# First stage of a fused block: rows scaled before a plain transpose, two blocks' columns formed by TensorE, filler products, another order of transfers

## The chip, the cores and the metric

The kernel runs on one core of a Trainium2 chip. The time is that of one execution on the device in microseconds. Five engines run their own instruction streams and meet at semaphores: TensorE (matrix products; its weight loads are listed apart), VectorE, ScalarE, GpSimd (POOL in the views), and SyncE (SP), which here only issues transfers.

## What is computed

One layer of a network on 1024 tokens of width 1024, float32. The first stage, the only one that the change touches, is the normalised input with a modulation computed from the condition `c`, times the first projections:

```python
mod = silu(c) @ ada_w + ada_b
sh1, sc1, g1, sh2, sc2, g2 = split(mod, 6)
h = rms_norm(x) * (1.0 + sc1) + sh1
y = mlstm_mixer(h, ml_w_in, ml_b_if, ml_norm_w, ml_w_out)
x = x + g1 * y
h = rms_norm(x) * (1.0 + sc2) + sh2
x = x + g2 * swiglu(h, ffn_w_gate_up, ffn_w_down)
out = rms_norm(x) * final_norm_w
```

`mlstm_mixer` projects `h` to queries, keys, values, an output gate and eight gate columns for four heads, runs a chunked recurrence and projects back.

## The kernel before, in words

The program is written out by hand: every engine has its own list of instructions, and the order in each list is the order of the code. Waits are explicit (`wait_ge` on a semaphore). Nothing is planned at run time. Transfers of the first stage are issued by SP in the order of its code and share the same DMA engines; a few small ones go out from ScalarE's and POOL's own queues.

The first stage works on eight rows of x (128 tokens by 1024 columns each, tile `xin`) and on eight blocks `k` of 128 columns of the transposed input (`xnT`, 128 columns by 1024 tokens, in two halves of 512 tokens).

- **Rows.** For row t ScalarE squares it and adds up (`square`, L916), copies a transposed bank of row t-2 out of PSUM (`evac_xT`, L926), and takes the root (`root`, L920). VectorE takes the reciprocal (`inverse`, L1402) and multiplies the identity by it (`diagonal`, L1418, tile `diag`, two buffers). TensorE then multiplies the row by the diagonal, eight products of 128 by 128 into two banks (L2136): it scales and transposes at once. VectorE copies the other bank out (`evac_xT`, L1423). A bank pair is used again two rows later.
- **Columns.** Block k needs a scale and a shift for each of its 128 columns of h: `silu(c) @ ada_w` for two sets of 128 columns. The weights of block k are one tile `ada0` of 1 MB (128 by 8 by 256, four buffers). VectorE multiplies its eight slices by the entries of `cact` and adds them (`sum1`, L1387, L1394, L1398, nine operations into `acc0`), and TensorE adds up over the partitions by two products with a column of ones (`mod_columns`, L2122). ScalarE adds the bias (`mod_columns`, L934). The sums of blocks 0 and 1 are spread between VectorE's rows, those of blocks 2 to 7 follow the rows.
- **Modulation.** ScalarE applies the columns to each half of block k (`modulate`, L944) and rounds it to the short float32 form that TensorE takes in one pass (`hH`, L948); POOL subtracts to get the rest (`hL`, L729). Every later product is made of three: high by high, low by high, high by low.
- **First products.** For each block TensorE does for both halves two times three products (queries and keys of head 0, L2088) and two for the gate columns (L2162), 16 in all, and ahead of block k it forms the columns of block k+1. It begins when the rows are all transposed, the half block is there (`m_L`), POOL has the first half weight unit's parts (`w_L`, L716, L722) and the gates' weights (`wg_L`, L735, L737).

SP's order (L468 to L483): rows 0, 1, 2 of x; the tile of block 0; rows 3 to 6; the tile of block 1; the gates' weights; row 7; the first half of weight unit 0; the tiles of blocks 2 and 3; the second half of unit 0; and then the tiles 4 to 7, each when its buffer is free (L464). `c` itself is loaded from ScalarE's queue (L908). A tile's buffer is free when VectorE's sum over it is done.

The wait that orders a row's part on TensorE is on the diagonal; on its banks, on both copies of two rows before:

```python
for t in range(NT):
    pe.wait_ge(n_hn, t + 1)
    for j in range(2):
        if t >= 2:
            pe.wait_ge(xT_ok[j], t - 1)
```

Of the kernel before, what the change touches and what calls it, by code (L numbers as in the profile page):

```python
# [21 lines left out]
ALU = mybir.AluOpType  # L22
ACT = mybir.ActivationFunctionType

P = 128
D = 1024
S = 1024
NT = S // P
KD = D // P
# [16 lines left out]
N1 = KD + 1  # L46
GATE_ROWS = 36
N_FOLDED = 7

# [79 lines left out]
def build(nc, x, c_col, ada_first, ada_first_b, ada_rest, ada_rest_b, w_units, w_gates, b_if, norm_w, final_w, out,  # L129
          scan_rows, mod_rows):  # L130
    with ExitStack() as ctx:
# [49 lines left out]
        th = at("th", [P, 2, DV], Z0 + 6144)  # L181
        diag = at("diag", [P, 2, P], Z0 + 6144)
        gate = at("gate", [P, 2, DV], Z0 + 8192)
# [270 lines left out]
        def _(sp):  # L454
# [7 lines left out]
            def ada_first_tile(k):  # L462

                if k >= 4:  # L464
                    sp.wait_ge(acc0_ok, N1 * (k - 3))
                sp.dma_start(ada0[:, k % 4], ada_first[k]).then_inc(ada0_in[k % 4], 16)

            for t in range(NT):  # L468
                sp.dma_start(xin[:, t, :], x[t]).then_inc(x_in[t], 16)
                if t == 2:  # L470
                    ada_first_tile(0)
                if t == 6:
                    ada_first_tile(1)
                    sp.dma_start(wg_raw[:], w_gates).then_inc(wg_in, 16)
            load_unit(0, (0,))
            for k in range(2, KD):
                ada_first_tile(k)
                if k == 3:
                    load_unit(0, (1,))
                if k == 6:  # L480
                    load_unit(1, (0,))
# [215 lines left out]
        def _(pool):  # L697
# [28 lines left out]
            def low1(k, half):  # L726
# [3 lines left out]
                                        ALU.subtract).then_inc(m_L, 1)  # L730

            pool.wait_ge(wg_in, 16)
            pool.wait_ge(wg_zero, 1)
# [3 lines left out]
            nc.gpsimd.tensor_tensor(wgL, wg_raw[:], wgH.bitcast(F32), ALU.subtract).then_inc(wg_L, 1)  # L737
            first_high()
            for c in range(4):
                first_low(c)  # L740
            for k in range(KD):
                for half in range(2):
                    low1(k, half)
                    if 3 <= 2 * k + half <= 6:
                        first_low(1 + 2 * k + half)
            pool.wait_ge(acc0_ok, N1 * KD)

# [148 lines left out]
        def _(act):  # L896
# [10 lines left out]

            act.dma_start(craw[:], c_col).then_inc(c_in, 16)  # L908
            act.dma_start(b1[:], ada_first_b).then_inc(b1_in, 16)
# [40 lines left out]
            for t in range(NT):  # L950
                act.wait_ge(x_in[t], 16)
                if t:
                    act.wait_ge(n_ms, t)
                square(t, xin[:, t, :])
                if t >= 2:
                    evac_xT(t - 2)
                root(t)
            act.wait_ge(b1_ok, 1)
            mod_columns(0)
            modulate(0, 0)  # L960
            evac_xT(NT - 2)
            evac_xT(NT - 1)
            modulate(0, 1)
# [399 lines left out]
        def _(dve):  # L1363
# [12 lines left out]
            def sum1(k, first=0, last=KD):  # L1376

                base = k * N1
                even, odd = (SUM_BANK[:, i * 2 * P:(i + 1) * 2 * P] for i in range(2))
                if first == 0:  # L1380
                    dve.wait_ge(ada0_in[k % 4], 16 * (k // 4 + 1))
                    if base:
                        dve.wait_ge(acc0_ok, base)
                for r in range(first, last):
                    acc1 = (even, odd)[r % 2]
                    if r < 2:
                        nc.vector.tensor_scalar(acc1, ada0[:, k % 4, r, :], cact[:, r:r + 1], None,  # L1387
                                                ALU.mult).then_inc(acc0_ok, 1)
                    else:
                        dve.wait_ge(acc0_ok, base + r - 1)  # L1390
                        if r == KD - 1 and k >= 2:
                            dve.wait_ge(mod1_mm, k - 1)
                        dst = acc0[:, k % 2, :] if r == KD - 1 else acc1
                        nc.vector.scalar_tensor_tensor(dst, ada0[:, k % 4, r, :], cact[:, r:r + 1], acc1,  # L1394
                                                       ALU.mult, ALU.add).then_inc(acc0_ok, 1)
                if last == KD:
                    dve.wait_ge(acc0_ok, base + KD)
                    nc.vector.tensor_tensor(acc0[:, k % 2, :], acc0[:, k % 2, :], even, ALU.add).then_inc(acc0_ok, 1)  # L1398
# [15 lines left out]

            def diagonal(t):
                if t >= 2:
                    dve.wait_ge(n_tr, 2 * (t - 1))
                nc.vector.tensor_scalar(diag[:, t % 2, :], ident[:], rstd[:, t:t + 1], None, ALU.mult).then_inc(n_hn, 1)  # L1418

            def evac_xT(t):  # L1420

                dve.wait_ge(n_tr, 2 * t + 2)
                nc.vector.tensor_copy(four_of(xnT, 1, t),  # L1423
                                      XT_BANKS[2 * (t % 2) + 1][:].rearrange("p (k n) -> p k n",
                                                                             n=P)).then_inc(xT_ok[1], 1)

# [5 lines left out]
            for t in range(NT):  # L1432
                inverse(t)
                diagonal(t)
                if t >= 2:
                    evac_xT(t - 2)
                if 1 <= t <= 3:
                    sum1(0, 3 * (t - 1), min(3 * t, KD))
                if t >= 5:
                    sum1(1, 2 * (t - 5), 2 * (t - 4))  # L1440
            sum1(1, 6)
            evac_xT(NT - 2)
            evac_xT(NT - 1)
            for k in range(2, KD):
                sum1(k)
# [638 lines left out]
        def _(pe):  # L2084
# [31 lines left out]
            def mod_columns(k):  # L2116

                pe.wait_ge(acc0_ok, N1 * (k + 1))
                if k:
# [6 lines left out]
            def start():  # L2126

                pe.wait_ge(set_ok, 3)
                pe.wait_ge(const_ok, 5)
                for t in range(NT):  # L2130
                    pe.wait_ge(n_hn, t + 1)
                    for j in range(2):
                        if t >= 2:
                            pe.wait_ge(xT_ok[j], t - 1)
                        for k in range(4):
                            ins = nc.tensor.matmul(XT_BANKS[2 * (t % 2) + j][:, k * P:(k + 1) * P],  # L2136
                                                   xin[:, t, (4 * j + k) * P:(4 * j + k + 1) * P], diag[:, t % 2, :],
                                                   start=True, stop=True)
                        ins.then_inc(n_tr, 1)
                    if t == 4:  # L2140
                        mod_columns(0)
                mod_columns(1)
                pe.wait_ge(wg_L, 1)
                ws = unit_weights(0, 2 * DK)
                for k in range(KD):
# [4 lines left out]
                    for half in range(2):  # L2150
# [5 lines left out]
                        for m in range(2):  # L2156
                            ins = three(QK_BANKS[2 * half + m][:], tuple(w[:, k, m * DK:(m + 1) * DK] for w in ws),
                                        hs, k, k, last)
                            if last:
                                ins.then_inc(qk_mm, 1)  # L2160
                        for i in range(2):
                            ins = nc.tensor.matmul(OP[half][:], gate_weights[:, k, :], hs[i], start=(k == 0 and i == 0),  # L2162
# [387 lines left out]
```

## Time and profile before

| | |
|---|---|
| median of 3 runs | 1089.62 us (1089.36 to 1090.15) |
| the profiled execution, its own time | 1089.08 us |
| its span, first to last instruction | 1087.30 us |
| TensorE busy | 1072.2 us (99%) |
| VectorE, ScalarE, POOL busy | 728.5, 447.4, 167.8 us |
| mean DMA rate over the span | 165 GB/s |

Busy time of an engine over the whole span says little here, since the stages differ. The chain of waits follows the work that ended last back to the start; the timelines give each engine's instructions in order with the idle time ahead of them and what ended it; the windows view gives busy time and transfer rate of a stretch. A row "x16" is sixteen instructions taken together, and its duration reaches from the first start to the last end.

### The profile page before, as it was taken

The page shows a single profiled execution, that of the slowest core. Times are in us where ns is not written, and L with a number is a line of the kernel's source. Part 1 is how long each engine was busy: PE and PEld are TensorE (multiplying, and loading weights), DVE is VectorE, ACT ScalarE, POOL GpSimd, SP SyncE. Part 2 cuts the span into 40 slices and gives each one's busy share as a digit, 9 for nine tenths or more (in the row PEclk, how much of TensorE's full clock was granted, in tenths as well). Part 3 has the DMA queues.
Part 4 walks back from the last instruction along what each step waited for, and adds up shares of the span by engine and source line. Part 5 has one row for each costly group of instructions (what it writes and reads, how often), then busy time and mean ns, then how long its engine had stood idle before and what let it go on. Part 6 is the DMA issues. An engine that isn't in the chain of part 4 may idle for free.

```text
span 1087.3 us, 14704 instructions
## 1 busy us (share of the span) xinstructions
PE 1072.2 (99%) x5139; PEld 901.3 (83%) x5139; DVE 728.5 (67%) x1289; ACT 447.4 (41%) x824; POOL 167.8 (15%) x149
## 2 busy tenths in 40 slices
PE   6999999999999999999999999999999999999997
PEld 6888888888888888888888888888888888888886
DVE  6846777477478627888666676756667465844666
ACT  7852232322234216754343333334333325444435
POOL 3752221212326423310000000000000000000000
PEclk9999999999999999999999999999999999999999
DMA  9425453532543423115536435453643879665544
GB/s 377 171 78 170 127 189 97 150 126 59 169 126 91 165 75 136 59 43 200 187 114 214 154 124 177 154 177 116 211 158 113 304 269 396 216 193 193 194 155 156
DMA packets 88091, 178.94 MB, mean 165 GB/s; under 512 B 8377, under 2 KB 31545, under 8 KB 86993
## 3 DMA queue, kind: packets, MB, share of 16 engines
q1 hardware_dynamic: 87104, 176.63, 48.3%
q0 software_dynamic: 480, 1.09, 0.3%
q8 instruction: 41, 0.67, 0.3%
q10 hardware_dynamic: 432, 0.27, 0.1%
q14 instruction: 34, 0.27, 0.1%
HBM read 135.97 MB, written 40.16 MB: 162 GB/s over the span
## 4 chain that ended last, share of the span: by engine, by line
PE 98%; DVE 1%; DMA 0%; ACT 0%; issue 0%; DVEq 0%
PE OP L2388 27%; PE OP L2088 21%; PE O L2388 15%; PE ST L2388 6%; PE DC L2388 5%; PE AD L2388 5%; PE O L2088 3%; PE ST L2088 3%; PE AD L2088 2%; PE DC L2088 2%; PE O L2245 1%; PE O L2261 1%; PE DC L2261 1%; PE ST L2136 1%; PE ST L2228 1%; PE OP L2162 1%
## 5 line engine op out<-in xcount | busy, mean ns | idle before, releaser
L1853 DVE TENSOR_TENSOR dL<-dF,dH 128x1024 fp32r<-128x1024 f32 x77 | 93.0, 1223 | 69.8 <-ACT dH L1235 69.1
L2088 PE MATMUL OP<-wH,hH 128*128 128x512 f32 (+1 forms) x360 | 135.0, 375 | 0.1
L2088 PE MATMUL OP<-wH,hL 128*128 128x512 f32 (+1 forms) x360 | 132.0, 367 | 0.0
L2088 PE MATMUL OP<-wL,hH 128*128 128x512 f32 (+1 forms) x360 | 131.7, 366 | 0.0
L1235 ACT CAST dH<-dF 128x1024 fp32r<-128x1024 f32 x77 | 79.8, 1051 | 89.1 <-DMA dF<-w_units 37.8
L2388 PE MATMUL OP<-tH,wsH 128*128 128x512 f32 x264 | 102.7, 389 | 0.0
L2388 PE MATMUL OP<-tL,wsH 128*128 128x512 f32 x264 | 102.7, 389 | 0.0
L2388 PE MATMUL OP<-tH,wsL 128*128 128x512 f32 x264 | 102.7, 389 | 0.0
L2088 PEld LDWEIGHTS OP<-wH,hL 128*128 128x128 f32 x360 | 67.8, 188 | 11.3
L2088 PEld LDWEIGHTS OP<-wH,hH 128*128 128x128 f32 x360 | 67.9, 189 | 10.3 <-issue 0.3
L2088 PEld LDWEIGHTS OP<-wL,hH 128*128 128x128 f32 x360 | 68.0, 189 | 10.0
L1147 ACT CAST wsH<-wsF 128x512 fp32r<-128x512 f32 x88 | 53.1, 620 | 47.3 <-DVE wsF L1769 39.9
L1147 ACT CAST wsH<-raw 128x512 fp32r<-128x512 f32 x66 | 38.8, 620 | 74.8 <-DMA raw<-w_units 58.6
L2388 PE MATMUL O<-hH,wsH 128*128 128x512 f32 x176 | 68.5, 389 | 0.0
L2388 PE MATMUL O<-hL,wsH 128*128 128x512 f32 x176 | 68.5, 389 | 0.0
L2388 PE MATMUL O<-hH,wsL 128*128 128x512 f32 x176 | 68.5, 389 | 0.0
L1808 DVE TENSOR_TENSOR wsL<-wsF,wsH 128x512 fp32r<-128x512 f32 x88 | 58.2, 686 | 14.4 <-ACT wsH L1147 14.4
L1764 DVE TENSOR_TENSOR wsF<-raw 128x512 f32<-128x512 f32 x21 | 14.5, 692 | 74.2 <-DMA raw<-w_units 64.8
L824 POOL TENSOR_TENSOR hg<-hc,gate 128x256 f32<-128x256 f32 x32 | 36.5, 1142 | 164.8 <-DVE gate L1597 164.8
L768 POOL DMA_DIRECT2D g2b<-mod_rows x1 | 0.6, 602 | 375.8 <-DVE wsL L1808 375.8
L2388 PEld LDWEIGHTS OP<-tH,wsL 128*128 128x128 f32 x264 | 49.6, 188 | 10.4
L2388 PEld LDWEIGHTS OP<-tL,wsH 128*128 128x128 f32 x264 | 49.5, 188 | 10.3
(344 smaller groups left out, 2642.2 us busy)
## 6 DMA issues: line engine op xcount, KB each, us to landing
raw<-w_units SPq DMA_DIRECT2D x76, 512.0 KB, 4.8
dF<-act_mid SPq DMA_DIRECT2D x77, 256.0 KB, 2.9
ada<-ada_rest SPq DMA_DIRECT2D x64, 256.0 KB, 2.9
wst<-w_units SPq DMA_DIRECT2D x44, 256.0 KB, 4.9
down_mid<-wst SPq DMA_DIRECT2D x22, 512.0 KB, 3.2
dF<-down_mid SPq DMA_DIRECT2D x44, 256.0 KB, 2.9
dF<-w_units SPq DMA_DIRECT2D x33, 256.0 KB, 5.6
ada<-ada_first SPq DMA_DIRECT2D x8, 1024.0 KB, 10.1
```

The source lines that it names most:

```text
L824: nc.gpsimd.tensor_tensor(hg[:, c - 1, h * DV:(h + 1) * DV], hc[:, (c - 1) % 2, :], gate[:, (c - 1) % 2, :], ALU.mult).then_inc(hg_ok, 1)
L1147: nc.scalar.copy(wsH[n % 2][W_SLOT.index(q)][:], src).then_inc(c_H, 1)
L1235: nc.scalar.copy(dH[g][:], dF[g][:]).then_inc(d_H, 1)
L1764: nc.vector.tensor_tensor(f[5][:], gate_up_block(0, 1), gate_up_block(1, 1), ALU.add).then_inc(c_sum, 1)
L1808: nc.vector.tensor_tensor(wsL[n % 2][i][:], src, wsH[n % 2][i][:].bitcast(F32), ALU.subtract).then_inc(c_L, 1)
L1853: nc.vector.tensor_tensor(dL[g][:], dF[g][:], dH[g][:].bitcast(F32), ALU.subtract).then_inc(d_L, 1)
L2088: ins = nc.tensor.matmul(out_ap, lhs[a], rhs[b], start=(n == 0 and i == 0), stop=(last and i == 2))
L2136: ins = nc.tensor.matmul(XT_BANKS[2 * (t % 2) + j][:, k * P:(k + 1) * P], xin[:, t, (4 * j + k) * P:(4 * j + k + 1) * P], diag[:, t % 2, : ...
L2162: ins = nc.tensor.matmul(OP[half][:], gate_weights[:, k, :], hs[i], start=(k == 0 and i == 0), stop=(last and i == 1))
L2228: nc.tensor.matmul(ST[c % 2][:, 0:P], kT[:, toks], qT[:, toks], start=True, stop=True)
L2261: ins = nc.tensor.matmul(out_ap, lhs[a], rhs[b], start=(first and i == 0), stop=(i == 2))
L2388: ins = nc.tensor.matmul(out_ap, lhs[a], rhs[b], start=(first and i == 0), stop=(last and i == 2), skip_group_check=True)
```

## The change

Six edits, all in the first stage:

1. `c` is loaded first on SP's queue and no longer from ScalarE's. SP then loads rows 0 to 5, the tile of block 0, rows 6 and 7, the first half of unit 0, the gates' weights, the tiles of blocks 1 and 2, the second half of unit 0, and the tiles of blocks 3 to 7.
2. VectorE multiplies the whole row by the reciprocal in place (`scale_row`), and TensorE transposes it plainly; the tile `diag` is gone.
3. The columns of blocks 0 and 1 come from TensorE alone (`columns_from_weights`): for each of a block's two sets eight products, the weight tile's slices as stationary operand and one column of `cact` as the moving one. The sets of block 0 stand behind rows 4 and 5, both of block 1 behind row 7. VectorE's sums begin with block 2, and the semaphore counts are shifted by two blocks.
4. TensorE multiplies a tile of ones by itself, 14 times ahead of row 0 and twice behind rows 0 to 3 and row 6 (`keep_warm`); nothing reads the results.
5. ScalarE's copies of a bank stand behind the root and stop at row 4; VectorE copies both banks of rows 5 to 7. VectorE's copies belong to row t-1 instead of t-2.
6. POOL splits the half unit before the gates' weights, and TensorE waits for the gates' weights only ahead of the first gate product.

```diff
+BY_PE = 2
+X_BY_ACT = 5
+WARM = 14
+FILL = 2
...
             def ada_first_tile(k):
-                if k >= 4:
-                    sp.wait_ge(acc0_ok, N1 * (k - 3))
+                if k >= 4 + BY_PE:
+                    sp.wait_ge(acc0_ok, N1 * (k - 3 - BY_PE))
+                elif k >= 4:
+                    sp.wait_ge(mod1_mm, k - 3)
                 sp.dma_start(ada0[:, k % 4], ada_first[k]).then_inc(ada0_in[k % 4], 16)
+            sp.dma_start(craw[:], c_col).then_inc(c_in, 16)
             for t in range(NT):
                 sp.dma_start(xin[:, t, :], x[t]).then_inc(x_in[t], 16)
-                if t == 2:
+                if t == 5:
                     ada_first_tile(0)
-                if t == 6:
-                    ada_first_tile(1)
-                    sp.dma_start(wg_raw[:], w_gates).then_inc(wg_in, 16)
             load_unit(0, (0,))
-            for k in range(2, KD):
+            sp.dma_start(wg_raw[:], w_gates).then_inc(wg_in, 16)
+            for k in range(1, KD):
                 ada_first_tile(k)
-                if k == 3:
+                if k == 2:
                     load_unit(0, (1,))
...
+            first_high()
+            for c in range(4):
+                first_low(c)
             pool.wait_ge(wg_in, 16)
...
-            first_high()
-            for c in range(4):
-                first_low(c)
...
-            act.dma_start(craw[:], c_col).then_inc(c_in, 16)
...
                 square(t, xin[:, t, :])
-                if t >= 2:
+                root(t)
+                if 2 <= t <= X_BY_ACT + 1:
                     evac_xT(t - 2)
-                root(t)
             act.wait_ge(b1_ok, 1)
             mod_columns(0)
             modulate(0, 0)
-            evac_xT(NT - 2)
-            evac_xT(NT - 1)
             modulate(0, 1)
...
-            def diagonal(t):
-                if t >= 2:
-                    dve.wait_ge(n_tr, 2 * (t - 1))
-                nc.vector.tensor_scalar(diag[:, t % 2, :], ident[:], rstd[:, t:t + 1], None, ALU.mult).then_inc(n_hn, 1)
+            def scale_row(t):
+                nc.vector.tensor_scalar(xin[:, t, :], xin[:, t, :], rstd[:, t:t + 1], None, ALU.mult).then_inc(n_hn, 1)
...
             for t in range(NT):
                 inverse(t)
-                diagonal(t)
-                if t >= 2:
-                    evac_xT(t - 2)
-                if 1 <= t <= 3:
-                    sum1(0, 3 * (t - 1), min(3 * t, KD))
-                if t >= 5:
-                    sum1(1, 2 * (t - 5), 2 * (t - 4))
-            sum1(1, 6)
-            evac_xT(NT - 2)
-            evac_xT(NT - 1)
-            for k in range(2, KD):
+                scale_row(t)
+                if t:
+                    if t - 1 >= X_BY_ACT:
+                        evac_xT(t - 1, 0)
+                    evac_xT(t - 1, 1)
+            evac_xT(NT - 1, 0)
+            evac_xT(NT - 1, 1)
+            for k in range(BY_PE, KD):
                 sum1(k)
...
+                def columns_from_weights(k, m):
+                    pe.wait_ge(ada0_in[k], 16)
+                    pe.wait_ge(c_act, 1)
+                    if k:
+                        pe.wait_ge(mod1_ok, 2 * k)
+                    for r in range(KD):
+                        ins = nc.tensor.matmul(DC[:, 2 * k + m:2 * k + m + 1], ada0[:, k, r, m * P:(m + 1) * P],
+                                               cact[:, r:r + 1], start=(r == 0), stop=(r == KD - 1))
+                    if m == 1:
+                        ins.then_inc(mod1_mm, 1)
+                def keep_warm(n):
+                    for _ in range(n):
+                        nc.tensor.matmul(OP[0][:, 0:P], ones[:], ones[:], start=True, stop=True)
+                keep_warm(WARM)
                 for t in range(NT):
                     pe.wait_ge(n_hn, t + 1)
...
-                            ins = nc.tensor.matmul(XT_BANKS[2 * (t % 2) + j][:, k * P:(k + 1) * P],
-                                                   xin[:, t, (4 * j + k) * P:(4 * j + k + 1) * P], diag[:, t % 2, :],
-                                                   start=True, stop=True)
+                            ins = nc.tensor.transpose(XT_BANKS[2 * (t % 2) + j][:, k * P:(k + 1) * P],
+                                                      xin[:, t, (4 * j + k) * P:(4 * j + k + 1) * P], ident[:])
                         ins.then_inc(n_tr, 1)
-                    if t == 4:
-                        mod_columns(0)
-                mod_columns(1)
-                pe.wait_ge(wg_L, 1)
+                    if t in (4, 5):
+                        columns_from_weights(0, t - 4)
+                    elif t < NT - 1:
+                        keep_warm(FILL)
+                for m in range(2):
+                    columns_from_weights(1, m)
```

What the edits do to the order on the engines shows at three places. First TensorE from row 4 to the first product. `ST` and `O` are the banks of the transposed rows, `DC` the bank of the columns, `OP` that of the fillers. Before:

```order
L2136 MATMUL ST<-diag,xin 128x128 x8
L2122 MATMUL DC<-ones,acc_75 128x1 x2
L2136 MATMUL O<-diag,xin 128x128 x8
L2136 MATMUL ST<-diag,xin 128x128 x8
L2136 MATMUL O<-diag,xin 128x128 x8
L2122 MATMUL DC<-ones,acc_75 128x1 x2
L2088 MATMUL O<-hH,wH 128x512
```

Now:

```order
L2152 MATMUL ST<-ident,xin 128x128 x8
L2135 MATMUL DC<-cact,ada_55 128x1 x8
L2152 MATMUL O<-ident,xin 128x128 x8
L2135 MATMUL DC<-cact,ada_55 128x1 x8
L2152 MATMUL ST<-ident,xin 128x128 x8
L2143 MATMUL OP<-ones 128x128 x2
L2152 MATMUL O<-ident,xin 128x128 x8
L2135 MATMUL DC<-cact,ada_55 128x1 x16
L2086 MATMUL O<-hH,wH 128x512
```

The two products per block with ones became sixteen per block with the weights, and they stand between the rows and ahead of the first product. Second SP's transfers up to the tiles that wait (`xin` rows of x, `ada_55` the tiles of the blocks, `raw` half weight units). Before:

```order
L469 DMA xin<-x 128x1024 x3
L466 DMA ada_55<-ada_first 128x2048
L469 DMA xin<-x 128x1024 x4
L466 DMA ada_55<-ada_first 128x2048
L474 DMA wg_raw<-w_gates 128x288
L469 DMA xin<-x 128x1024
L460 DMA raw<-w_units 128x1024
L466 DMA ada_55<-ada_first 128x2048 x2
L460 DMA raw<-w_units 128x1024
```

Now:

```order
L473 DMA craw<-c_col 128x8
L475 DMA xin<-x 128x1024 x6
L471 DMA ada_55<-ada_first 128x2048
L475 DMA xin<-x 128x1024 x2
L463 DMA raw<-w_units 128x1024
L479 DMA wg_raw<-w_gates 128x288
L471 DMA ada_55<-ada_first 128x2048 x2
L463 DMA raw<-w_units 128x1024
```

The tile of block 0 moved behind rows 3 to 5, that of block 1 behind row 7, half a unit and the gates. Third VectorE at the end of the rows and the first whole sum. Before:

```order
L1402 RECIPROCAL rstd<-sd 128x1
L1418 TENSOR_SCALAR diag<-ident,rstd 128x128
L1423 COPY xnT<-O 128x4x128
L1394 SCALAR_TENSOR_TENSOR AD<-ada_55,cact,AD 128x256 x3
L1394 SCALAR_TENSOR_TENSOR acc_75<-ada_55,cact,AD 128x256
L1398 TENSOR_TENSOR acc_75<-acc_75,AD 128x256
L1423 COPY xnT<-ST 128x4x128
L1423 COPY xnT<-O 128x4x128
L1387 TENSOR_SCALAR AD<-ada_55,cact 128x256 x2
```

Now:

```order
L1403 RECIPROCAL rstd<-sd 128x1
L1417 TENSOR_SCALAR xin<-xin,rstd 128x1024
L1424 COPY xnT<-ST 128x4x128 x2
L1424 COPY xnT<-O 128x4x128 x2
L1388 TENSOR_SCALAR AD<-ada_55,cact 128x256 x2
```

The sums between the rows are gone, and two more copies stand behind the last row.

## Rows read from the trace of the kernel before

**Rows 1.** Chain of waits that ended last, page, whole program, share by engine.

```profile
PE 98%; DVE 1%; DMA 0%; ACT 0%; issue 0%; DVEq 0%
```

**Rows 2.** TensorE's timeline: start, duration (us), line, operation, count.

```profile
8.62 3.75 PE L2136 MATMUL ST<-diag,xin 128*128 128x128 f32 x16 [8.62 <-DVE diag L1418]
...
21.78 1.95 PE L2136 MATMUL ST<-diag,xin 128*128 128x128 f32 x16
23.57 1.95 PE L2136 MATMUL O<-diag,xin 128*128 128x128 f32 x16
...
26.07 0.48 PE L2088 MATMUL O<-hH,wH 128*128 128x512 f32 x1
...
30.84 0.48 PE L2088 MATMUL O<-hH,wH 128*128 128x512 f32 x1
...
34.58 0.50 PE L2122 MATMUL DC<-ones,acc 128*128 128x1 f32 x4
34.94 0.49 PE L2088 MATMUL O<-hH,wH 128*128 128x512 f32 x1
```

**Rows 3.** Weight loads' timeline, same columns; in brackets the idle time before.

```profile
28.18 0.19 PEld L2088 LDWEIGHTS ST<-hH,wH 128*128 128x128 f32 x1 [0.47 <-POOL hL L729]
...
30.37 0.52 PEld L2122 LDWEIGHTS DC<-ones,acc 128*128 128x128 f32 x4 [0.49 <-DVE acc L1398]
```

**Rows 4.** ScalarE's timeline, first rows of x.

```profile
4.77 0.21 ACT L911 ACTIVATE cact<-craw 128x8 f32<-128x8 f32 x1 [1.80 <-DMA craw<-c_col]
...
6.40 1.04 ACT L916 ACTIVATE junk<-xin 128x1024 f32<-128x1024 f32 x1
...
7.56 0.29 ACT L920 ACTIVATE sd<-ms,eps 128x1 f32<-128x1 f32 x1
7.76 1.04 ACT L916 ACTIVATE junk<-xin 128x1024 f32<-128x1024 f32 x1
...
10.71 0.59 ACT L926 COPY xnT<-ST 128x512 f32<-128x512 f32 x1 [0.44 <-PE ST L2136]
11.19 0.30 ACT L920 ACTIVATE sd<-ms,eps 128x1 f32<-128x1 f32 x1
```

**Rows 5.** DMA issues near 0.8 and 6.8 us: KB, us to landing.

```profile
xin<-x SPq DMA_DIRECT2D x1, 512.0 KB, 3.8
craw<-c_col ACTq DMA_DIRECT2D x1, 4.0 KB, 4.0
...
ada<-ada_first SPq DMA_DIRECT2D x1, 1024.0 KB, 17.6
```

**Rows 6.** Windows view, 12.2 to 26: length, engines' busy time, PEclk, DMA, GB/s.

```profile
12.20:26.00 13.80, 13.71 (x121) 13.52 (x120) 12.80 (x33) 11.81 (x27) 6.29 (x8) 1.00 1.03 418
```

**Rows 7.** SP's timeline of DMA issues.

```profile
0.75 1.35 SPq L469 DMA_DIRECT2D xin<-x  x3
...
6.75 1.43 SPq L466 DMA_DIRECT2D ada<-ada_first  x2
```

**Rows 8.** VectorE's timeline: a diagonal, first operations of sums 2 and 3.

```profile
8.19 0.29 DVE L1418 TENSOR_SCALAR diag<-ident,rstd 128x128 f32<-128x128 f32 x1
...
26.66 0.86 DVE L1387 TENSOR_SCALAR AD<-ada,cact 128x256 f32<-128x256 f32 x2
...
30.43 0.87 DVE L1387 TENSOR_SCALAR AD<-ada,cact 128x256 f32<-128x256 f32 x2
```

**Rows 9.** Line view of the later scaling of rows: min, median, max ns.

```profile
L1945 DVE TENSOR_SCALAR xs<-x,rstd x8: 753/754/1033, 409.2 to 452.8; 128x1024 f32<-128x1024 f32 x8
```

**Rows 10.** TensorE's timeline, later plain transposes, four each.

```profile
418.05 0.60 PE L2112 MATMUL O<-ident,xs 128*128 128x128 f32 x4
418.49 0.60 PE L2112 MATMUL ST<-ident,xs 128*128 128x128 f32 x4
```

**Rows 11.** POOL's timeline: half unit's cast, first low half of block 0.

```profile
20.32 1.04 POOL L716 CAST wH<-raw 128x1024 fp32r<-128x1024 f32 x1 [1.24 <-DMA raw<-w_units]
...
24.19 1.27 POOL L729 TENSOR_TENSOR hL<-xnT,hH 128x512 fp32r<-128x512 f32 x1
```

More of the change, by code:

```diff
@@ L181, in build @@
         th = at("th", [P, 2, DV], Z0 + 6144)
-        diag = at("diag", [P, 2, P], Z0 + 6144)
         gate = at("gate", [P, 2, DV], Z0 + 8192)
@@ L745, in _ @@
                         first_low(1 + 2 * k + half)
-            pool.wait_ge(acc0_ok, N1 * KD)
+            pool.wait_ge(acc0_ok, N1 * (KD - BY_PE))
             nc.gpsimd.memset(rows[0:GATE_ROWS, A_, :], 0.0).then_inc(rows_set, 1)
@@ L1376, in sum1 @@
             def sum1(k, first=0, last=KD):
-                base = k * N1
+                base = (k - BY_PE) * N1
                 even, odd = (SUM_BANK[:, i * 2 * P:(i + 1) * 2 * P] for i in range(2))
@@ L1390, in sum1 @@
                         dve.wait_ge(acc0_ok, base + r - 1)
-                        if r == KD - 1 and k >= 2:
+                        if r == KD - 1 and k >= 2 + BY_PE:
                             dve.wait_ge(mod1_mm, k - 1)
@@ L1413, in low, with evac_xT @@
                                             ALU.subtract).then_inc(n_L, 1)
-            def diagonal(t):
-                if t >= 2:
-                    dve.wait_ge(n_tr, 2 * (t - 1))
-                nc.vector.tensor_scalar(diag[:, t % 2, :], ident[:], rstd[:, t:t + 1], None, ALU.mult).then_inc(n_hn, 1)
[L1420 to L1425, printed above, removed]
+            def scale_row(t):
+                nc.vector.tensor_scalar(xin[:, t, :], xin[:, t, :], rstd[:, t:t + 1], None, ALU.mult).then_inc(n_hn, 1)
+            def evac_xT(t, j):
+                dve.wait_ge(n_tr, 2 * t + j + 1)
+                if j == 0 and t == X_BY_ACT:
+                    dve.wait_ge(xT_ok[0], t)
+                nc.vector.tensor_copy(four_of(xnT, j, t),
+                                      XT_BANKS[2 * (t % 2) + j][:].rearrange("p (k n) -> p k n",
+                                                                             n=P)).then_inc(xT_ok[j], 1)
             dve.wait_ge(b1_in, 16)
@@ L2116, in mod_columns @@
             def mod_columns(k):
-                pe.wait_ge(acc0_ok, N1 * (k + 1))
+                pe.wait_ge(acc0_ok, N1 * (k + 1 - BY_PE))
                 if k:
@@ L2160, in start @@
                                 ins.then_inc(qk_mm, 1)
+                        if k == 0 and half == 0:
+                            pe.wait_ge(wg_L, 1)
                         for i in range(2):
```

## The prediction

> **What bounds the kernel now.** The chain of waits comes first: 98% of it is TensorE [rows 1], so a microsecond counts only where TensorE's own sequence starts sooner or loses a gap. TensorE's timeline of the start [rows 2] shows where that can be. It stands until 8.62 us, transposes eight rows until 25.5, starts the first product at 26.07, and from 30.84 repeats a period of 4.10 us (30.84 to 34.94), block after block. Two gaps lie between [rows 3]: 0.47 us for POOL's low half of block 0, and 0.49 us for VectorE's sum of block 2, whose columns so come at 30.37. Sixteen products with no gap take 3.74 us (30.84 to 34.58) against the 4.30 from 26.07 to 30.37: 0.56 of gap. What is won or lost before 30.37 is what the kernel wins or loses, as long as the period behind it stays.
>
 ScalarE waited for the transposes (0.44 us at 10.71) [rows 4]: the eight rows are bound by TensorE now.
>
> **The change, part by part.** All times are of the profiled execution (span 1087.30, 1089.08 in all; the median of the runs is 0.54 above it).
>
> *The start.* I call s the start of ScalarE's first Square, 6.40 now. It came 1.63 us after the Silu at 4.77, which waited for c [rows 4]; c took 4.0 us from its issue on ScalarE's queue [rows 5]. Now SP sends c first and the rows after it. What an almost empty transfer takes at the head of SP's queue no row shows. Bounds: row 0 of x landed in 3.8 us [rows 5] with 0.52 MB, which at 418 GB/s [rows 6] is 1.25 us of data, leaving 2.5; above, the 4.0 as before. I take 2.5, as it is from this queue and place: issued at 0.75 [rows 7], c is there at 3.25, and s would be 4.88. But row 0 is now issued one DMA later (1.35 us for three [rows 7], 0.45), so 4.55 becomes 5.0, and **s = 5.0**; the other end is 6.4.
>
> *ScalarE's pace.* Square to root start is 1.16 us, root 0.20, a bank's copy 0.48 [rows 4]. Copies now stand behind the root, after rows 2 to 6 only. Root 4 thus starts at s + 5×1.16 + 4×0.20 + 2×0.48 = s + 7.56.
>
> *VectorE.* It loses the sums of blocks 0 and 1 (3.77 us a block, 26.66 to 30.43 [rows 8]), which stood between the rows, and scales whole rows in place of a diagonal. The same operation on a full row occurs later in the kernel: 0.75 us, once 1.03 [rows 9]. From the first root's start (7.56) to TensorE's first pass (8.62) it was 1.06 with the diagonal's 0.29 in it [rows 2, 4, 8]; with 0.75 it is 1.52. TensorE gets row 4 at **s + 9.1**.
>
> *TensorE.* A plain transpose is one pass: four took 0.44 us (418.05 to 418.49 [rows 10]), so 0.88 a row. Half the columns of a block are 8 products of one column, 16 passes. No row shows 16; four cost 0.36 (34.58 to 34.94) to 0.47 (30.37 to 30.84) [rows 2, 3], 0.09 to 0.117 a pass. I take the rows' 0.112, since these passes load the same 128 by 128 float32 weights: 1.79 a set, ends 1.44 and 1.87. Two fillers are four passes, 0.45. The 14 opening ones wait only for POOL's constants. With 16 of their 28 passes at the lower level like the first row's, they take 3.75 + 12×0.112 = 5.1 us; begun before 2.6 they end before row 0 is scaled (s + 1.16 + 1.52 = 7.7). Later ones would delay row 0 alone, for rows 0 to 3 need 0.88 + 0.45 in pitches of 1.36 to 1.84. From row 4 on TensorE is full: four rows, four sets, one pair of fillers, 4×0.88 + 4×1.79 + 0.45 = 11.1 us. First product: s + 9.1 + 11.1 = **25.2**, against 26.07.
>
> *What must be there by then.* From row 0 at 5.0 by bytes at 418 GB/s: block 0's tile of ada (five rows and 1.05 MB behind) at 13.8, asked for at s + 10.0 = 15.0; rows 6 and 7 at 15.1 and 16.3, their Squares at 15.1 and 16.9; the half unit at 17.5; block 1's tile at 20.4, asked for at 21.6. POOL needs 3.87 for the half unit (20.32 to 24.19) and 1.27 for the first low half [rows 11]: 22.6, with 2.6 us of room for the gates, which it now does in between. Row 7 is transposed by 21.6; before, the way from the last transposes (25.5) to the second half's product (28.18) was 2.7 us [rows 2, 3], and that product is now asked for at 27.0. Block 2's tile, issued at 6.75, lands 17.6 later at 24.4 [rows 5, 7]; the bytes ahead of it are the same. Its sum, 3.77, is ready at 28.2 and asked for at 25.2 + 3.74 = 28.94. So both gaps of [rows 3] are covered, the later by 0.7 us.
>
> *Later.* VectorE's 3.77 a block stays below TensorE's 4.10. Tile 4 may be loaded sooner, but the queue ahead of it is as long. Everything else waits for what it waited for. I cost this at nothing; its cover is that difference of 0.33 us a block, and a tile that came late would stop TensorE for its whole delay.
>
> **Sum.** Block 2's columns at 28.94 instead of 30.37: 1.43 us, 0.87 by the earlier first product and 0.56 by the gaps. 1089.62 − 1.43 = **1088.2**.
>
> **A rule that would make it more.** [Rows 10] say that a plain transpose halves a row's time. The Trainium skill (TensorE: Matmul & The Clock Gate, section Terms) gives transpose mode as four times faster for float32. A row would then be about 0.45, an estimate from that page, and the last four rows would save 1.7 us more, up to the limit of the second rival. The trace disagrees: it shows 0.88 against 1.79.
>
> **The rivals.**
> *TensorE at the lower level (7%, ends slower).* Place: row 4 to the first product, 32 + 64 + 4 = 100 passes, 0.11 us more each at the lower level. More than 13 slow passes eat the 1.43; more than 33 make the kernel slower by over 0.2%. A ramp as at the start (16 passes) gives 1088.2 + 1.8 = 1090.0; all 100 give 1099.2. For it: between rows 0 and 3 TensorE now stands up to 0.5 us per row, and the trace has no such stretch. Against: the fillers, and that the gaps of 0.5 in [rows 3] left the 4.10 period behind them as it was. The Trainium skill (same page, section What's actually happening) holds that the throttled state is the default and that activity lifts it. By that rule the fillers would lift it before row 0, and too little activity would bring it back; the trace agrees with the lifting ([rows 2]) and shows no return.
>
> *Shorter columns, stopped by the sum (20%).* At 0.09 a pass the 64 passes save 1.4 us, but the sum of block 2 at 28.2 then stops TensorE: the gain is at most 30.37 − 28.2 = 2.1 us, 1087.5. For it: the 0.36; against it: the 0.47 and the row's 0.112. Only if that tile lands sooner too does it go beyond 0.2%.
>
> *c is no sooner (17%).* If its 4.0 us was latency and not the sharing with x, s stays 6.4, the first product comes at 26.6, block 2's columns at 30.3, and only the gaps pay for it: 1089.6. For it: c and row 0 were issued together and landed alike (4.0, 3.8). Against: c has 4 KB, the row 512.
>
> **How the numbers follow.** About 0.2% (2.2 us) is what a measurement of this kernel can tell from no change. The forecast has 56%: 1088.2, give or take 0.4. Faster by over 0.2% needs the second rival with an earlier tile, or a gain that I do not see: 17%. Slower by over 0.2% is the first rival beyond 33 passes, or a tile late by more than 3.6 us: 7%. The rest, 76%, is within. The range goes from 1087.0 (second rival, tile 0.5 sooner) to 1090.0 (third rival, or one ramp).
>
> **What would show it.** Right: first Square near 5.0; row 4's transposes near 14.1; rows of 0.88 and sets of 1.8; no TensorE pause from row 4 to the first product at 25.2; block 2's columns near 28.9; the period still 4.10. Wrong: passes of 0.2 us after row 4 (first rival); passes near 0.09 and a pause before block 2's columns (second); a first Square at 6.4 (third); a pause for ada or POOL before the first product; a gain or loss that arises after 31 us.

## The result and the profile after

The change made the kernel **slower**: median 1094.69 us over 10 runs (1090.58 to 1097.44), against 1089.22 for the kernel before over 10 runs (1088.02 to 1090.15). The ratio is 1.0050 (95% interval 1.0037 to 1.0062). The time lies outside the forecast's range of 1087.0 to 1090.0, and the change is beyond the 0.2% that counts as none. The single times are spread over 7 us where those of the kernel before are spread over 2, and they go with the mean granted clock of TensorE:

```
us                 1090.58  1092.23  1092.42  1093.60  1094.07  1095.31  1095.54  1097.33  1097.37  1097.44
mean granted clock   0.996    0.994    0.994    0.992    0.992    0.991    0.992    0.989    0.989    0.989
```

The profiled execution of before has 0.999. The profiled execution of the change is the fastest of the ten, so its trace shows the effect at its smallest: +1.50 us against the profiled execution of before (1090.58 to 1089.08).

The chain of waits is what it was [rows 1], TensorE from end to end:

```profile
PE 98%; ACT 1%; DMA 0%; DVE 0%; issue 0%; SPq 0%
```

ScalarE's timeline of the start (start, duration, engine, line, operation, in brackets the idle time before and what ended it), which answers to [rows 4]:

```profile
2.49 0.21 ACT L914 ACTIVATE cact<-craw 128x8 f32<-128x8 f32 x1
...
5.07 1.06 ACT L919 ACTIVATE junk<-xin 128x1024 f32<-128x1024 f32 x1 [0.85 <-DMA xin<-x]
```

The Silu of `c` is at 2.49 and waits for nothing; the first Square is at 5.07 and waits for row 0 of x. The forecast had 5.0.

TensorE's timeline from row 4 on, same columns, which answers to [rows 2]:

```profile
14.01 1.09 PE L2152 MATMUL ST<-ident,xin 128*128 128x128 f32 x8 [0.30 <-DVE xin L1417]
14.94 1.84 PE L2135 MATMUL DC<-cact,ada 128*128 128x1 f32 x16
16.65 1.07 PE L2152 MATMUL O<-ident,xin 128*128 128x128 f32 x8
17.56 1.84 PE L2135 MATMUL DC<-cact,ada 128*128 128x1 f32 x16
19.26 1.69 PE L2152 MATMUL ST<-ident,xin 128*128 128x128 f32 x8
20.74 1.06 PE L2143 MATMUL OP<-ones 128*128 128x128 f32 x4
21.59 1.72 PE L2152 MATMUL O<-ident,xin 128*128 128x128 f32 x8
23.15 3.87 PE L2135 MATMUL DC<-cact,ada 128*128 128x1 f32 x32
26.87 0.77 PE L2086 MATMUL O<-hH,wH 128*128 128x512 f32 x1
...
27.87 0.63 PE L2086 MATMUL O<-hH,wL 128*128 128x512 f32 x1
28.30 0.63 PE L2086 MATMUL ST<-hH,wH 128*128 128x512 f32 x1
...
30.39 0.39 PE L2086 MATMUL ST<-hL,wH 128*128 128x512 f32 x1
30.61 0.40 PE L2086 MATMUL ST<-hH,wL 128*128 128x512 f32 x1
...
31.99 0.50 PE L2120 MATMUL DC<-ones,acc 128*128 128x1 f32 x4
...
36.12 0.50 PE L2120 MATMUL DC<-ones,acc 128*128 128x1 f32 x4
```

From 14.01 there is no bracket, so TensorE does not stand once; both gaps of [rows 3] are closed. Rows 4 and 5 take 0.93 and 0.91, a column set 1.71. Rows 6 and 7, of the same eight transposes, take 1.48 (19.26 to 20.74) and 1.56. The first products start 0.43 apart (27.87 to 28.30), from about 30 on 0.22 (30.39 to 30.61). Block 2's columns come at 31.99 instead of 30.37, 1.62 later; the period behind them is 4.13. So the whole loss of this execution arises before 32 us, on a TensorE that waits for nothing from row 4 on.

The windows view of that stretch (from:to, length, busy time and count of TensorE, its weight loads, VectorE, ScalarE, POOL, then TensorE's granted clock, DMA share, GB/s):

```profile
16.30:19.70 3.40, 3.40 (x33) 3.40 (x33) 2.98 (x7) 2.41 (x9) 1.77 (x3) 0.98 1.07 433
19.74:23.15 3.41, 3.41 (x19) 3.41 (x17) 2.25 (x4) 1.61 (x4) 3.33 (x5) 0.53 0.97 398
23.15:26.56 3.41, 3.41 (x33) 3.41 (x31) 3.04 (x8) 1.43 (x2) 2.79 (x3) 0.98 1.06 436
26.57:29.97 3.40, 3.40 (x11) 2.78 (x11) 3.26 (x9) 2.82 (x6) 0.93 (x1) 0.52 0.96 378
30.00:60.00 30.00, 30.00 (x145) 24.98 (x144) 19.90 (x46) 22.81 (x41) 21.93 (x21) 1.00 0.37 141
```

Twice the granted clock is at half, the lower of the two levels (1.2 GHz). The shares of 0.98 and 0.53 put the edges 0.1 to 0.2 us ahead of the windows': from about 19.6 to 23.0, right behind the two sets of block 0, and from about 26.4 to 29.8, from the last passes of the two sets of block 1 on. TensorE is busy for the whole of both stretches and of those ahead of them. The first makes rows 6 and 7 and the fillers slow, the second the end of the sets and the first seven products. Before, TensorE's clock has no such stretch from 12.2 to 26 [rows 6], nor from there to 60:

```profile
26.00:60.00 34.00, 33.90 (x164) 27.80 (x165) 26.48 (x62) 27.18 (x50) 25.67 (x24) 1.00 0.49 181
```

For the very start the view can't be used: it reads 1.00 there too (before, 8.62 to 10.00), over passes of 0.23 us. There the duration of the passes tells the level.

### The profile page after: what moved, and what is told of

Read it like the earlier page. It is cut to its first block, busy times and chain, and to the rows that moved or that the text cites. A ratio compares the mean times of both kernels' runs of the same rounds, so it can differ in the third digit from the quotient of the medians.

```text
span 1088.7 us, 14759 instructions
## 1 busy us (share of the span) xinstructions
PE 1079.4 (99%) x5179; PEld 908.4 (83%) x5179; DVE 726.3 (67%) x1274; ACT 446.3 (41%) x821; POOL 169.6 (16%) x149
## 4 chain that ended last, share of the span: by engine, by line
PE 98%; ACT 1%; DMA 0%; DVE 0%; issue 0%; SPq 0%
PE OP L2407 27%; PE OP L2086 21%; PE O L2407 16%; PE ST L2407 5%; PE DC L2407 5%; PE AD L2407 5%; PE O L2086 4%; PE ST L2086 4%; PE AD L2086 2%; PE DC L2086 2%; PE O L2264 1%; PE O L2280 1%; PE DC L2280 1%; PE OP L2181 1%; PE ST L2247 1%; PE DC L2135 1%
## 5 line engine op out<-in xcount | busy, mean ns | idle before, releaser
L2407 PEld LDWEIGHTS OP<-tH,wsH 128*128 128x128 f32 x264 | 49.6, 188 | 10.4
```

The costliest lines, as they stand in the source:

```text
L2407: ins = nc.tensor.matmul(out_ap, lhs[a], rhs[b], start=(first and i == 0), stop=(last and i == 2), skip_group_check=True)
```

## The experiments

Two theories. **A**: TensorE's column sets, whose passes each stream a single column, bring the clock down although TensorE never stands; what comes next pays. **B**: it is the other half of the edit, the short plain transposes with pauses between rows 0 to 4, and fillers that are too few. Under A the rest of the forecast should hold once the sets are made wide. The expectations also have a theory **C**: the loss has nothing to do with the clock, and the low stretches only go along with it.

**1. Sets of 128 columns.** The same passes with the same weights, but each streams 128 copies of the column of `cact`. 128 columns of the bank are written in place of one, and only the first is kept.

```diff
-                        ins = nc.tensor.matmul(DC[:, 2 * k + m:2 * k + m + 1], ada0[:, k, r, m * P:(m + 1) * P],
-                                               cact[:, r:r + 1], start=(r == 0), stop=(r == KD - 1))
+                        ins = nc.tensor.matmul(DC[:, 2 * k + m:2 * k + m + WIDE], ada0[:, k, r, m * P:(m + 1) * P],
+                                               cact[:, r:r + 1].to_broadcast([P, WIDE]), start=(r == 0), stop=(r == KD - 1))
```

> The changed kernel with one edit: the column products stream 128 copies of the column of cact in place of one, with the same 64 passes and weight loads. Theory A (passes that stream a single column count as little activity, so TensorE's clock falls behind them): no stretch at 1.2 GHz after the opening one, sets still 1.8 us each, first product near 25.2 us, block 2's columns near 28.9, 1.0 to 1.9 us faster than the kernel before, runs within about 1 us of each other. Theory B (the pauses between the rows, or the plain transposes, bring the clock down): the same low stretches as in the changed kernel, 2 to 8 us slower than before. Theory C (the loss has nothing to do with the clock's level, the low stretches only go along): low stretches gone, time still 2 to 8 us above before.

Measured: median 1087.64 (11 runs, 1087.19 to 1088.79) against 1089.19 for the kernel before (21 runs); ratio 0.9986 (0.9977 to 0.9995), faster by 1.55 us. Every run has a mean clock of 0.998 to 1.000. TensorE's timeline and the windows view of this kernel:

```profile
14.08 1.09 PE L2153 MATMUL ST<-ident,xin 128*128 128x128 f32 x8 [0.31 <-DVE xin L1418]
15.01 1.95 PE L2136 MATMUL DC<-cact,ada 128*128 128x128 f32 x16
...
19.45 1.03 PE L2153 MATMUL ST<-ident,xin 128*128 128x128 f32 x8
...
22.00 3.84 PE L2136 MATMUL DC<-cact,ada 128*128 128x128 f32 x32 [0.19 <-DMA ada<-ada_first]
25.59 0.48 PE L2087 MATMUL O<-hH,wH 128*128 128x512 f32 x1
...
29.33 0.50 PE L2121 MATMUL DC<-ones,acc 128*128 128x1 f32 x4
```

```profile
6.00:26.00 20.00, 18.92 (x163) 18.00 (x162) 15.72 (x31) 15.80 (x36) 7.89 (x9) 1.00 1.03 419
26.00:60.00 34.00, 34.00 (x171) 28.62 (x170) 24.68 (x57) 27.45 (x49) 25.35 (x24) 1.00 0.48 187
```

A wide set takes little longer than a narrow one (16 passes reach over 1.95 us against 1.84). Behind row 4 TensorE now even waits once (0.19 us, for block 1's tile), and the clock stays up. This edit alone turns a loss of 0.5% into a gain of 0.14%. A holds, and with the low stretches the loss is gone too, so C falls.

**2. The sets alone, in the kernel before.** Blocks 0 and 1 by one-column sets; rows by the diagonal as before, no plain transposes, no fillers, transfers in the old order. VectorE's sums of blocks 0 and 1 are gone and the semaphore counts shifted, as in the change; the piece shown is TensorE's.

```diff
-                    if t == 4:
-                        mod_columns(0)
-                mod_columns(1)
+                    if t in (4, 5):
+                        columns_from_weights(0, t - 4)
+                for m in range(2):
+                    columns_from_weights(1, m)
```

> The kernel before with only the columns of blocks 0 and 1 moved to TensorE (products of one column), rows still multiplied by the diagonal, no fillers, transfers as before. TensorE's rows have no pauses here and no plain transposes. 64 passes of 0.112 less the 8 of the old columns are 6.3 us more work on TensorE, of which the gaps give 0.56 back. Theory A: a stretch at 1.2 GHz follows the two sets of block 1, 6 to 10 us slower than before in all. Theory B: clock at 2.4 GHz from about 12.5 us on, 5.7 us slower.

Measured: 1096.24 (4 runs, 1095.91 to 1099.62), ratio 1.0070 (1.0054 to 1.0087). Most of that is plain work: four sets in place of eight passes stand on an already full TensorE (some 1.7 us each at the full clock), with no row made cheaper; the expectation puts this at 5.7 us, and the median is 7.05 above before. But the clock falls as well. The windows view of its profiled execution, the one of 1099.62, the slowest of the four (the others have mean clocks of 0.997, against 0.999 before, and no trace):

```profile
25.50:29.40 3.90, 3.90 (x37) 3.90 (x37) 0.69 (x1) 2.92 (x6) 1.27 (x1) 1.00 0.69 233
29.50:32.00 2.50, 2.50 (x25) 2.50 (x23) 2.31 (x6) 1.35 (x2) 1.04 (x1) 0.96 0.22 92
32.03:38.85 6.82, 6.82 (x23) 5.81 (x23) 6.54 (x17) 4.12 (x7) 2.74 (x4) 0.52 0.53 190
```

and TensorE's timeline there:

```profile
29.49 4.71 PE L2135 MATMUL DC<-cact,ada 128*128 128x1 f32 x32
34.06 0.77 PE L2086 MATMUL O<-hH,wH 128*128 128x512 f32 x1
```

Block 1's two sets run from 29.49 to 34.06. The clock falls inside them, at about 31.8, and stays low over the first products until about 38.6. With no plain transposes and no fillers in the program, B cannot explain it. The sets between rows 4 to 6 left no low stretch in this execution (25.50 to 29.40 at 1.00), where the rows around them have twice as many passes.

**3. Wide sets without fillers.** Experiment 1 with this edit:

```diff
-WARM = 14
-FILL = 2
+WARM = 0
+FILL = 0
```

> The first of these (128 copies) without any filler product. If the fillers are what lifts the clock before the rows, it rises only after several us of rows, rows 0 to 3 take 1.7 us each instead of 0.88, which still fits ScalarE's pitch of 1.36 to 1.84, and the first product comes at 25.2 to 27; a rise as late as row 6 costs 2 us. If the pauses between unfilled rows keep the clock low (theory B), it stays at 1.2 GHz to the first product: first product at about 36, 9 us slower than before.

Measured: 1087.55 (10 runs, 1086.61 to 1089.26), ratio 0.9987 (0.9978 to 0.9997), the same as with the fillers. TensorE's timeline of the start, and a window behind it:

```profile
7.86 1.94 PE L2153 MATMUL ST<-ident,xin 128*128 128x128 f32 x8 [7.86 <-DVE xin L1418]
...
13.14 1.09 PE L2153 MATMUL O<-ident,xin 128*128 128x128 f32 x8
14.67 1.09 PE L2153 MATMUL ST<-ident,xin 128*128 128x128 f32 x8 [0.43 <-DVE xin L1418]
```

```profile
12.50:60.00 47.50, 46.95 (x283) 41.04 (x282) 35.95 (x78) 37.16 (x70) 33.58 (x33) 1.00 0.63 252
```

Row 0 is slow (1.94 for eight transposes), row 3 is not; behind 12.5 the clock stays up in spite of a pause of 0.43 ahead of row 4. Short transposes and pauses alone did not bring it down: B falls as the cause by itself. Row 4 comes 0.59 us later than with fillers, but the last pair of fillers is gone from the full stretch, and the times are the same: beside wide sets the fillers buy nothing.

**4 and 8. The change again, two more executions.** The kernel as it is, no edit, since the first profile was that of the fastest run.

> The changed kernel unaltered, once more, for the profile of another execution, since its runs lie between 1090.6 and 1097.4. Theory A: stretches at 1.2 GHz again, each of the same length as the two seen (3.41 us), beginning during or right behind the column sets, their number and place another, and the time above 1088 by about half of their sum. Theory C: low stretches as before whatever the time.

> The changed kernel unaltered, a third profile, to see where the low stretches of a slower execution lie. Theory A: they begin between 17 and 27 us, each a multiple of 3.41 us long, and reach into products of 512 columns; nothing low after some 60 us; the time above 1087.6 is 0.4 to 0.5 of the low stretches' sum. Theory C: the low stretches are as in the first profile even if the time is several us more.

Measured: 1091.85 both times. The windows view of the first:

```profile
19.18:22.59 3.41, 3.41 (x18) 3.41 (x18) 2.44 (x3) 1.84 (x4) 3.39 (x5) 0.50 1.00 411
...
26.00:32.83 6.83, 6.83 (x20) 5.67 (x21) 6.55 (x17) 4.13 (x7) 3.71 (x4) 0.50 1.00 384
```

with its first product in TensorE's timeline:

```profile
27.25 0.77 PE L2086 MATMUL O<-hH,wH 128*128 128x512 f32 x1
```

and the windows view of the second:

```profile
19.70:25.16 5.46, 4.92 (x44) 4.68 (x43) 3.47 (x6) 3.28 (x6) 5.38 (x8) 0.98 1.01 416
25.19:32.01 6.82, 6.82 (x23) 5.81 (x24) 6.68 (x17) 4.13 (x7) 3.61 (x3) 0.52 1.00 368
```

The low stretch that begins inside block 1's sets is twice as long as in the first profile, over 512-column products that leave TensorE no gap. In the second of the two block 0's sets bring nothing down. Same program, three executions, three patterns. The time above experiment 1's 1087.6 was expected at 0.4 to 0.5 of the low stretches' sum. It is 0.41 in the first (4.2 of 10.24 us) and 0.62 in the second (4.2 of 6.82), a miss: there row 4 starts 0.3 us later and TensorE waits 0.55 for block 1's tile. Of the times up to 1097.44 only the mean clock is known, since none of those executions was profiled.

**5. `c` by ScalarE's queue again**, on top of experiment 1:

```diff
-            sp.dma_start(craw[:], c_col).then_inc(c_in, 16)
...
+            act.dma_start(craw[:], c_col).then_inc(c_in, 16)
```

> The kernel with 128 copies of the column, and c loaded from ScalarE's queue again (one part of the change undone; SP then begins with row 0). If c's place at the head of SP's queue is what starts the rows 1.4 us sooner, the first Square goes back to 6.2 to 6.5, the first product comes at 26.5 to 27.0, and the time is 1.0 to 1.4 us above that of the first experiment (1088.6 to 1089.1). If it does not matter, the first Square stays at 5.1 and the time at 1087.6.

Measured: 1088.64 (11 runs), before 1089.44 (27 runs), ratio 0.9996 (0.9987 to 1.0005). ScalarE's timeline:

```profile
4.82 0.21 ACT L915 ACTIVATE cact<-craw 128x8 f32<-128x8 f32 x1 [1.85 <-DMA craw<-c_col]
...
6.45 1.04 ACT L920 ACTIVATE junk<-xin 128x1024 f32<-128x1024 f32 x1
```

and in TensorE's timeline block 2's columns:

```profile
30.21 0.50 PE L2121 MATMUL DC<-ones,acc 128*128 128x1 f32 x4
```

Silu and first Square are back where they were in [rows 4], and the columns come at 30.21, 0.88 later than in experiment 1 and only 0.16 sooner than before. By the times, `c` at the head of SP's queue is worth 1.00 us between the medians of the two experiments, and 0.75 with each against its own kernel before (gains of 0.80 and 1.55). That is half of the gain of experiment 1 or more; the gain of experiment 5 itself is not clear of noise (0.9987 to 1.0005).

**6 and 7. One block's sets wide.** On top of experiment 1, `wide` is 128 for block 0 alone (6) or for block 1 alone (7), and 1 for the other:

```diff
+                    wide = WIDE if k == 0 else 1
```

> The changed kernel with 128 copies of the column for block 0's two sets alone; block 1's two sets, 3.6 us in one piece right ahead of the first product, stream one column. If a piece of such passes as long as this is enough (theory A in its plain form), one or more stretches at 1.2 GHz fall on the first products, and the time is 1089 to 1096 with a spread of several us. If it takes all four sets, no low stretch and 1087.6.

> The counterpart: 128 copies for block 1's sets alone; block 0's two sets of 1.8 us stream one column, with eight transposes of a row between them and after them. If short pieces between rows are enough, stretches at 1.2 GHz fall on rows 6 and 7 and block 1's sets, the first product comes 1 to 4 us later than 25.6, and the time is 1088.5 to 1092. If only the long piece does it, no low stretch and 1087.6.

Measured for 6: 1089.64 (10 runs, 1089.09 to 1092.16), ratio 1.0008 (0.9999 to 1.0017), mean clocks of 0.995 to 0.998 in all ten. TensorE's timeline and the windows view:

```profile
25.79 0.48 PE L2087 MATMUL O<-hH,wH 128*128 128x512 f32 x1
...
26.80 0.55 PE L2087 MATMUL ST<-hL,wH 128*128 128x512 f32 x1
27.15 0.63 PE L2087 MATMUL ST<-hH,wL 128*128 128x512 f32 x1
```

```profile
23.00:27.00 4.00, 4.00 (x32) 3.82 (x32) 2.33 (x6) 1.60 (x4) 2.94 (x3) 0.98 1.01 419
27.04:30.46 3.42, 3.42 (x10) 2.61 (x10) 3.28 (x10) 3.08 (x5) 2.43 (x2) 0.53 1.02 424
```

Block 1's sets end at 25.79 at the full clock, four products run at the full clock, and only then, at about 26.9, during the product that starts at 26.80, does it fall: 1.1 us after the last narrow pass.

Measured for 7: 1090.88 (10 runs, 1087.44 to 1092.94), ratio 1.0013 (1.0002 to 1.0025). The profiled execution is the one of 1087.44 and has no low stretch:

```profile
13.00:26.00 13.00, 12.47 (x109) 11.95 (x108) 10.44 (x21) 8.94 (x20) 7.90 (x9) 1.00 1.03 417
```

Eight of the other nine have mean clocks of 0.994 to 0.997 and 1089.45 to 1092.94. So, by the mean clocks, block 0's sets, split by a row, bring the clock down in most executions and not in all; no trace shows one of those. Each half costs some of the time. Each kernel against its own kernel before: +0.20 us with block 1's sets narrow, +1.44 with block 0's, +5.47 with both (the change), and −1.55 with none. So the two add 1.75 and 2.99 apart, and 7.02 together, more than their sum; nothing here shows why, and the two further executions of the change (1091.85) lie only 4.2 above experiment 1.

Experiments 1 and 3 beat both kernels, by about 1.6 us against before and 7 us against the change.

## Why the prediction was wrong

**The step that failed** is in the prediction's part on TensorE: the column sets were priced by their duration alone ("I take the rows' 0.112, since these passes load the same 128 by 128 float32 weights"), and all of "four rows, four sets, one pair of fillers" was then put at the upper level of the clock. The duration of a set was right: 1.71 against 1.79. What was missed is that such passes lower the clock for the work behind them.

Point by point:

- First Square 5.0: measured 5.07. Row 4 at 14.1: 14.01. Plain rows 0.88: 0.91 and 0.93. Right.
- First product 25.2: 26.87; with wide sets 25.59, of which 0.19 is a wait for block 1's tile. From row 4 to the first product that is 12.86 us against 11.51. **1.35 us lost to the clock.**
- Block 2's columns 28.94: 31.99; with wide sets 29.33. Between first product and columns, 5.12 us against 3.74. **1.38 us more lost to the clock.** Together 2.73 of the 2.96 us between these two profiled executions (1090.58, 1087.62). The wait of 0.19 stands in the one with wide sets alone, so the clock cost somewhat more than the difference shows.
- Both gaps closed, and the period stayed (4.13, forecast 4.10): right. VectorE's sum of block 2 was done at about 28.1 (below), forecast 28.2:

```profile
27.66 0.42 DVE L1399 TENSOR_TENSOR acc<-acc,AD 128x256 f32<-128x256 f32 x1
```

- The gain of 1.43 us, for a kernel whose clock stays up: the mechanism was right, the size in part luck. In experiment 1 block 2's columns come at 29.33, 1.04 sooner than before and not 1.43. The 0.39 that is missing is there at the first product already (25.59 for 25.2). At least 0.19 of it is the wait for block 1's tile, which was forecast to be there at 20.4 and asked for at 21.6, and which TensorE had at 22.00. That the medians are 1.55 apart, and the profiled executions 1.46, owes 0.31 to a place that the prediction does not have. TensorE's timeline before, and then of experiment 1:

```profile
930.43 0.39 PE L2388 MATMUL O<-dH,dL 128*128 128x512 f32 x1
930.97 0.47 PE L2388 MATMUL O<-dH 128*128 128x512 f32 x1 [0.15 <-DVE sA L1865]
```

```profile
929.28 0.39 PE L2408 MATMUL O<-dH,dL 128*128 128x512 f32 x1
929.51 0.47 PE L2408 MATMUL O<-dH 128*128 128x512 f32 x1
```

  Before, TensorE stood there for VectorE's `sA`, and the two products start 0.54 apart; in experiment 1 they start 0.23 apart. The prediction named "a gain or loss that arises after 31 us" as a sign of being wrong, and this is one.

**The first rival** was the one that came, with another cause and a wider place than it had, and its 7% rested on those. It looked for a cause in the pauses between rows 0 to 3; experiment 3 has one of 0.43 behind them and no fillers, and keeps its clock. Its place was half right: it counted only the 100 passes up to the first product; half of the loss lies behind that, in 512-column products. What spoke against it, "that the gaps of 0.5 in [rows 3] left the 4.10 period behind them as it was", is true and tells nothing here: those were pauses amid wide passes, and this is work without a pause. The kernel before does have one-column passes, four at a time ahead of wide products [rows 3]. No row of it had sixteen or more in sequence, and that absence should have been treated like any other unknown price, with an end on the slow side.

On its rule: the Trainium skill (TensorE: Matmul & The Clock Gate, section HAM oscillation — how this bites in real kernels) puts a clock that falls amid a kernel down to stretches in which TensorE is idle. The trace differs: in 16.30 to 19.70 ahead of the first fall TensorE is busy for 3.40 of 3.40 us, and the measurement decides: here the clock fell on a TensorE that the profile counts as busy throughout. The prediction's words on the same page, that the trace shows no return to the lower level, held for the kernel before alone. The Trainium skill's rule on transpose mode (same page, section Terms) stays contradicted: a row took 0.91, not the 0.45 that was estimated from it.

**The third rival** (`c` no sooner) is refuted by the Silu at 2.49, and experiment 5 puts a price on it: 0.75 to 1.00 us, 0.88 at block 2's columns. **The second** (shorter columns, stopped by the sum) is refuted by sets of 1.71.

**What stays open.** What exactly lowers the clock was not mapped: no width between 1 and 128 was tried. Whether the plain transposes add to the falls behind block 0's sets was not tried by itself either; with rows by the diagonal, the one profile of experiment 2 has no fall there. Why one execution falls behind block 0's sets and another does not was not settled either, nor where the low stretches lie in the slowest executions, which no trace shows.

## What to carry to other kernels

Here eight products with one moving column last nearly as long as eight with 128 on the same weights (1.84 us against 1.95), but a sequence of them on a full TensorE can halve its clock for microseconds (3.4 to 6.8 in these traces), and the work behind it pays. Where such products can't be avoided, stream copies of the column beside it: that cost at most 0.1 us a set here. (Other, useful columns in their place were not tried.) When a profile shows TensorE without a gap and the same instruction at two durations, look at the granted clock by windows before looking for a wait, and take more than one profile when the mean clock differs from run to run.

## What the runs showed that was not expected

- The clock fell on a TensorE that had been busy without a pause, about 19.6 to 23.0 and 26.4 to 29.8 in the first profile, 26.0 to 32.8 in another. Wide products at full occupancy ran for up to 5.6 us (27.25 to 32.83) before it rose again.
- The fall can come after its cause has ended: 1.1 us after the last narrow pass in experiment 6.
- The mean over the span hides it: 0.996 against 0.999. But it orders the ten runs of the change almost perfectly, at about 1 us per 0.001.
- `c` (4 KB) at the head of SP's queue was there by 2.49 us, sooner than the 3.25 of the forecast, although the rows of x followed at once; from ScalarE's queue, beside them, it was awaited until 4.82.
